# Backward products on the off-diagonal quarters, first output tile by single merged tiles, second down unit split early

## The reference

```python
def step(s0, inp):                       # one token of one direction; the scan runs forward and reversed
    r_t, w_t, k_t, v_t, kk_t, a_t = inp
    sa = einsum("bhvk,bhk->bhv", s, -kk_t)
    s = s * w_t[:, :, None, :] + sa[..., None] * (kk_t * a_t)[:, :, None, :] + v_t[..., None] * k_t[:, :, None, :]
    return s, einsum("bhvk,bhk->bhv", s, r_t)

merged = sigmoid(ga) * (attn_o @ w_attn_br) + sigmoid(gr) * (rwkv_o @ w_rwkv_br)
x = x + gate1 * (merged @ w_out)
h2 = modulate(rmsnorm(x, norm2_g), shift2, scale2)
up_u, up_g = split(dwconv3(h2 @ ffn_up, ffn_conv), 2)
x = x + gate2 * ((silu(up_g) * up_u) @ ffn_down)
```

## Time and profile before

| | |
|---|---|
| median of 3 runs | 1376.88 us (1375.66 to 1378.38) |
| profiled execution | 1380.84 us, its span 1379.1 us |
| mean granted clock of TensorE | 0.977 |
| PE busy | 1294.0 us, 13903 records |
| DVE / ACT / POOL busy | 689.9 / 550.1 / 42.1 us |
| first pass of the recurrence | from 320.3 us |
| second pass of the recurrence | from 589.2 us |
| output projection | from 782.5 us |
| down units | from 1192.4 us |

### The profile page before, as it was taken

One profiled execution on the slowest core, in us unless ns is written; L12 is line 12 of the kernel. 1 busy time (PEld: TensorE's weight loads), 2 busy tenths in 40 slices (PEclk: granted clock), 3 DMA queues, 4 the chain that ended last, 5 costly groups with the idle time before them and its releaser, 6 DMA issues.

```text
span 1379.1 us, 31730 instructions
## 1 busy us (share of the span) xinstructions
PE 1294.0 (94%) x13903; PEld 1196.7 (87%) x13903; DVE 689.9 (50%) x1036; ACT 550.1 (40%) x864; POOL 42.1 (3%) x103
## 2 busy tenths in 40 slices
PE   4899999998999769899999899899999999899996
PEld 1899999997999545499989788799999999899995
DVE  3437642642544676565556412654545545434544
ACT  4645534422233477533342121733334333233433
POOL 0100011000010000010000000000000000000000
PEclk9999999999999998999999999999999999999998
DMA  9322365315000200011017574021221211022222
GB/s 389 143 71 102 110 271 180 105 45 209 8 5 4 92 1 1 0 53 34 8 41 259 225 294 177 31 88 65 64 88 61 91 61 46 23 66 71 69 76 92
DMA packets 24027, 131.70 MB, mean 96 GB/s; under 512 B 2896, under 2 KB 3664, under 8 KB 15344
## 3 DMA queue, kind: packets, MB, share of 16 engines
q1 hardware_dynamic: 19104, 103.98, 21.5%
q0 software_dynamic: 4816, 26.11, 5.0%
HBM read 111.74 MB, written 18.34 MB: 94 GB/s over the span
## 4 chain that ended last, share of the span: by engine, by line
PE 60%; DVE 3%; ACT 2%; issue 1%; DVEq 0%; ACTq 0%
PE ps L712 30%; PE ps L1206 11%; PE ps L882 2%; PE ps L870 2%; PE ps L1093 1%; PE ps L850 1%; PE ps L737 1%; PE ps L756 1%; PE ps L1069 1%; PE ps L999 1%; PE ps L747 1%; DVE nmax L1972 1%; PE ps L1070 1%; PE ps L862 1%; PE ps L1040 1%
## 5 line engine op out<-in xcount | busy, mean ns | idle before, releaser
L712 PE MATMUL ps<-h2lo,whi 128*128 128x322 f32 x672 | 154.5, 311 | 0.7 <-ACT facc L1308 0.7
L712 PE MATMUL ps<-h2hi,wlo 128*128 128x322 f32 x672 | 155.0, 312 | 0.0
L712 PE MATMUL ps<-h2hi,whi 128*128 128x322 f32 x672 | 154.0, 310 | 0.0
L1662 DVE TENSOR_TENSOR wlo<-raw,whi 128x2048 fp32r<-128x2048 f32 x47 | 107.5, 2288 | 70.4 <-ACT whi L1269 70.4
L712 PE MATMUL ps<-hlo,whi 128*128 128x322 f32 x544 | 127.9, 316 | 1.0 <-ACT qkv L1334 1.0
L712 PE MATMUL ps<-hhi,wlo 128*128 128x322 f32 x544 | 125.4, 312 | 0.0
L712 PE MATMUL ps<-hhi,whi 128*128 128x322 f32 x544 | 124.7, 310 | 0.0
L712 PEld LDWEIGHTS ps<-h2hi,whi 128*128 128x128 f32 x672 | 114.2, 190 | 0.0
L712 PEld LDWEIGHTS ps<-h2lo,whi 128*128 128x128 f32 x672 | 113.0, 189 | 0.9 <-DVE wlo L1662 0.9
L712 PEld LDWEIGHTS ps<-h2hi,wlo 128*128 128x128 f32 x672 | 113.6, 189 | 0.0
L1709 DVE SCALAR_TENSOR_TENSOR facc<-fraw,par,facc 128x642 f32<-128x642 f32 x44 | 39.0, 887 | 138.7 <-ACT facc L1308 138.7
(11 more groups left out here) (339 smaller groups left out, 2596.7 us busy)
## 6 DMA issues: line engine op xcount, KB each, us to landing
raw<-in_wblk SPq DMA_DIRECT2D x48, 1024.0 KB, 4.9
adl<-in_wada SPq DMA_DIRECT2D x8, 2048.0 KB, 7.9
raw<-in_wdn SPq DMA_DIRECT2D x44, 256.0 KB, 2.6
adaw<-in_wada SPq DMA_DIRECT2D x4, 2048.0 KB, 20.7
gate_scratch<-gout POOLq DMA_DIRECT2D x16, 322.0 KB, 2.5
gld<-gate_scratch POOLq DMA_DIRECT2D x8, 644.0 KB, 4.6
attention_inputs_used<-attention_scratch SPq DMA_DIRECT2D x1, 5056.0 KB, 15.5
u_scratch<-uout POOLq DMA_DIRECT2D x12, 320.0 KB, 2.4
```

What stands on the lines that cost most here:

```text
L712: mm = pe.matmul(o, w, v, start=first, stop=last and w is hi and x is xh[n])
L1662: TT(wlo[s][:, :], raw[s][:, :], whi[s][:, :].bitcast(F32), ALU.subtract).then_inc(lo_done, 1)
```

## The change

Three edits.

**The recurrence.** The backward direction's H, G1 to G4, P and U go to the two off-diagonal quarters. H of d = 1 is written to the other 64 partitions and to the pair's second bank, so its copy in `hm` lies swapped. G of d = 1 takes R from those partitions and writes back to its own; so does U with P. Since R must lie on the other partitions for that, `rm` gets a third slot, and ACT fills it with two copies of 64 partitions each (stages X0 to X4, after R0 and V1 to V4). G5 writes d = 1's result straight to the third slot, on the diagonal. The loops over q and d are turned, so that four matmuls in a row name four different quarters. H1 now waits for `AK` and not for `T0`, since H writes where KA stood, and G waits for ACT's X and not for DVE's V. P0 takes over the wait for the last Y1.

**The merge.** The first output tile is written out as `out_first`: each k-tile waits for its own `mlo`. It no longer waits for the last branch tile's reading before it starts; `ada_late(4)` moves ahead of the last k-tile. The other seven tiles are as before.

**The MLP.** The second down unit is split ahead of the last up block too, into spare halves of the buffers of s = 0 (`dhi_second`, `dlo_second`, columns 512 to 1023 of `whi[0]` and `wlo[0]`).

```diff
-        rm[s] += [sb(f"rm{s}_{g}", [P, 2, 2, CH]) for g in range(2)]
+        rm[s] += [sb(f"rm{s}_{g}", [P, 3, 2, CH]) for g in range(2)]
...
-    AC_ST = ["P0", "H1", "U0", "H2", "P1", "H3", "U1", "Y1", "H4", "TR", "H5"]
+    AC_ST = ["P0", "X0", "H1", "U0", "H2", "X1", "P1", "H3", "X2", "U1", "Y1", "H4", "X3", "TR", "H5", "X4"]
...
-                gp.tensor_copy(rm[s][g % 2][:, :, :, :].rearrange("p d q n -> p (d q) n"),
+                gp.tensor_copy(rm[s][g % 2][:, 0:2, :, :].rearrange("p d q n -> p (d q) n"),
...
             elif name[0] == "H":
                 l = int(name[1])
-                dv("T0" if l == 1 else f"C{l - 1}")
-                for d in range(2):
-                    for q in range(2):
-                        for r in half:
-                            mm = pe.matmul(bank(b1, CH, CH * (2 * d + q))[r], abm[s][g % 2][r, d, q, 0, :], tm[s][r, d, q, :],
-                                           start=True, stop=True)
+                dv("AK" if l == 1 else f"C{l - 1}")
+                for q in range(2):
+                    for d in range(2):
+                        for r, away in zip(half, half[::-1]):
+                            mm = pe.matmul(bank(b0 + d, CH, CH * q)[away if d else r], abm[s][g % 2][r, d, q, 0, :],
+                                           tm[s][r, d, q, :], start=True, stop=True)
             elif name[0] == "G":
                 l = int(name[1])
                 ac(f"H{l}")
-                dv("AK" if l == 1 else f"V{l - 1}")
-                for d in range(2):
-                    for q in range(2):
-                        for r in half:
-                            left, right = rm[s][g % 2][r, d, q, :], hm[s][r, d, q, :]
+                ac(f"X{l - 1}")
+                for q in range(2):
+                    for d in range(2):
+                        for r, away in zip(half, half[::-1]):
+                            at = away if d else r
+                            turned, right = rm[s][g % 2][at, 2 * d, q, :], hm[s][at, d, q, :]
                             if l == 5:
-                                left, right = right, left
-                            mm = pe.matmul(bank(b0, CH, CH * (2 * d + q))[r], left, right, start=True, stop=True)
+                                mm = pe.matmul(bank(b0, CH, 4 * CH + CH * (2 * d + q))[at], right, turned, start=True, stop=True)
+                            else:
+                                mm = pe.matmul(bank(b0 + d, CH, 2 * CH + CH * q)[r], turned, right, start=True, stop=True)
             elif name[0] == "P":
                 if q == 0:
                     ac("TR")
+                    if g > 0:
+                        if g - 1 in ADDED:
+                            dv("Y1", g - 1)
+                        else:
+                            ac("Y1", g - 1)
                     if g == 1:
                         pe.wait_ge(sl_done, it + 1)
                     elif g > 1:
                         dv("S1", g - 1)
                 else:
                     dv("S0")
-                for d in range(2):
-                    for r in half:
-                        mm = pe.matmul(bank(b2, CH, CH * d)[r], akm[s][g % 2][r, d, q, 0, :], vt64[s][r, chunk_of(g, d, q), :],
-                                       start=True, stop=first)
-                    if not first:
-                        for r in half:
-                            mm = pe.matmul(bank(b2, CH, CH * d)[r], ar[s][r, d, chunk_of(g, d, q), 0, :], state(q)[r, d, :],
-                                           start=False, stop=True)
+                    if g == NG - 1:
+                        pe.wait_ge(pe_g[s], at_stage(PE_ST, it, g, "Y0"))
+                for n in range(1 if first else 2):
+                    for d in range(2):
+                        for r, away in zip(half, half[::-1]):
+                            left, right = (ar[s][r, d, chunk_of(g, d, q), 0, :], state(q)[r, d, :]) if n else \
+                                (akm[s][g % 2][r, d, q, 0, :], vt64[s][r, chunk_of(g, d, q), :])
+                            mm = pe.matmul(bank(b2 + d, CH, 6 * CH)[away if d else r], left, right, start=n == 0,
+                                           stop=first or n == 1)
             elif name[0] == "U":
                 ac(f"P{q}")
                 if q == 0:
                     dv("V5")
                 for d in range(2):
-                    for r in half:
-                        mm = pe.matmul(bank(b2, CH, P + CH * d)[r], rm[s][g % 2][r, d, q, :], pw[s][r, d, :], start=True, stop=True)
+                    for r, away in zip(half, half[::-1]):
+                        at = away if d else r
+                        mm = pe.matmul(bank(b2 + d, CH, 7 * CH)[r], rm[s][g % 2][at, 2 * d, q, :], pw[s][at, d, :], start=True,
+                                       stop=True)
...
-        pe.wait_ge(tile_evac, 2 * BLK_OUT + 2)
-        ada_late(4)
-        pe.wait_ge(m_lo, KD)
+        def out_first():
+
+            pe.wait_ge(lo_done, BLK_OUT + 1)
+            pe.wait_ge(hi_done, BLK_OUT + 1)
+            pe.wait_ge(tile_evac, 2 * BLK_OUT + 1)
+            for k in range(KD):
+                if k == KD - 1:
+                    pe.wait_ge(tile_evac, 2 * BLK_OUT + 2)
+                    ada_late(4)
+                pe.wait_ge(m_lo, k + 1)
+                hi, lo = (w[BLK_OUT % 2][:, k * 256:k * 256 + P] for w in (whi, wlo))
+                for q, (w, x) in enumerate(((hi, mlo[k]), (lo, mhi[k]), (hi, mhi[k]))):
+                    for o, v in zip(out_halves(0), halves(x)):
+                        mm = pe.matmul(o, w, v, start=k == 0 and q == 0, stop=k == KD - 1 and q == 2)
+            mm.then_inc(tile_done, 1)
...
+        out_first()
+        between_out(0)
+        pe.wait_ge(tile_evac, 2 * BLK_OUT + 2)
+        dense_tile(BLK_OUT % 2, 1, range(KD), mhi, mlo, out_halves(2), 256).then_inc(tile_done, 1)
+        between_out(1)
+        for b in range(BLK_OUT + 1, BLK_UP):
...
+            second = k == 1 and n == 1
             pe.wait_ge(d_hi, n + 1)
             pe.wait_ge(d_lo, n + 1)
+            xh, xl = (dhi_second, dlo_second) if second else (dhi[s], dlo[s])
             for f in (2, 3, 0, 1) if k == 0 and not again else range(4):
-                hi, lo = whi[s][:, f * P:f * P + P], wlo[s][:, f * P:f * P + P]
+                at = (4 + f if second else f) * P
+                hi, lo = (w[0 if second else s][:, at:at + P] for w in (whi, wlo))
                 outs = out_halves(2 * f, TP - 2)
                 if again:
                     pe.wait_ge(d_evac, f + 1)
                 if k == 0 and not again and f < 2:
                     pe.wait_ge(tile_evac, 2 * NBLK + 1 + f)
-                for q, (w, x) in enumerate(((hi, dlo[s]), (lo, dhi[s]), (hi, dhi[s]))):
+                for q, (w, x) in enumerate(((hi, xl), (lo, xh), (hi, xh))):
...
             for g, name, s in paired(AC_ST):
                 b0, b1, b2, b3 = range(4 * s, 4 * s + 4)
-                ac.wait_ge(pe_g[s], at_stage(PE_ST, it, g, name))
-                if name[0] == "H":
-                    ins = ac.activation(hm[s][:, :, :, :].rearrange("p d q n -> p (d q n)"), bank(b1, 4 * CH), ACT.Copy)
+                if name[0] == "X":
+                    ac.wait_ge(dv_g[s], at_stage(DV_ST, it, g, "R0" if name == "X0" else "V" + name[1]))
+                    for r, away in ((slice(0, 64), slice(64, 128)), (slice(64, 128), slice(0, 64))):
+                        ins = ac.activation(rm[s][g % 2][away, 2, :, :].rearrange("p q n -> p (q n)"),
+                                            rm[s][g % 2][r, 1, :, :].rearrange("p q n -> p (q n)"), ACT.Copy)
+                else:
+                    ac.wait_ge(pe_g[s], at_stage(PE_ST, it, g, name))
+                if name[0] == "X":
+                    pass
+                elif name[0] == "H":
+                    ins = ac.activation(hm[s][:, :, :, :].rearrange("p d q n -> p d (q n)"), ps[:, b0:b0 + 2, 0:2 * CH], ACT.Copy)
                 elif name[0] in "PU":
-                    dst, at = (pw[s], 0) if name[0] == "P" else (uw[s], P)
-                    ins = ac.activation(dst[:, :, :].rearrange("p d n -> p (d n)"), bank(b2, P, at), ACT.Copy)
+                    dst, at = (pw[s], 6 * CH) if name[0] == "P" else (uw[s], 7 * CH)
+                    ins = ac.activation(dst[:, :, :], ps[:, b2:b2 + 2, at:at + CH], ACT.Copy)
...
+            second = first and s == 1
+            ac.activation(whi[0][:, 512:1024] if second else whi[s][:, 0:512], raw[s][:, 0:512], ACT.Copy)
+            ac.activation((dhi_second if second else dhi[s])[:, :], af[:, k, :], ACT.Copy).then_inc(d_hi, 1)
 
         up_block(NBLK - 2, FF - 2, 0, False, False)
-        ac.wait_ge(act_done, 1)
+        ac.wait_ge(act_done, 2)
         ac.wait_ge(tile_done, 2 * NBLK - 2)
         down_hi(0, 0, 0, True)
+        down_hi(1, 1, 1, True)
         up_block(NBLK - 1, FF - 1, 1, False, False)
-
         ac.wait_ge(act_done, FF)
-        ac.wait_ge(tile_done, 2 * NBLK)
```

(16 more changed lines are left out.)

25 lines of the change are left out of this document (12 added, 13 removed).

## The result

The changed kernel takes 1420.24 us (median of 4, 1418.59 to 1421.63); beside it the kernel before took 1377.63. The ratio is 1.030, with a 95% interval from 1.028 to 1.0321: **43 us slower**, where 4 us faster was forecast. The time lies outside the predicted range.

A forecast was written before the change was run, and what follows sets the result against it. PE's queue was taken to bound the recurrence. Recurrence +6.2, merge -5.7, down unit -6.2 and clock +1.4 gave -4.3 us, so 1372.6 from the median 1376.88; range 1366 to 1382.

The forecast's parts named there:

- Four quarters at once: Chunk products on PE: four quarters run together at 0.0146 us a record, halving 11.2 us a group to 5.6.
- A: Recurrence on PE: off-diagonal quarters don't run beside the diagonal ones; net +28 us, 1405; chance 10%.
- B: Recurrence on PE: matmuls issue no faster than one per 0.025 us; net +15 us, 1392; chance 6%.
- The chunk stages through ACT: Recurrence: G waits for ACT's copies of R; +1.3 us a second-pass group, about nothing in the first, +6.2 in all.
- the walk: Step-by-step sum of waits and stage lengths through one second-pass group, from KB to KB; total +1.3 us.
- G2 to S1: Second-pass group, levels 2 and 3: this stretch goes from 4.30 us to 3.33.
- For PE falling to half clock: Recurrence: PE, now idling up to 2 us at a time, drops to half clock here and there; +1.4 us.
- rival C: Recurrence clock: a fall costs 1.7, perhaps 1.2 us; from five falls no gain, with seven groups +3, 1380; chance 14%.
- last sign of being wrong: Recurrence: the forecast is wrong if its clock row is under 0.95.
- The merge, -5.7: First output tile: starts right behind the branch tiles; 4.0 us from the gap and 1.7 from the clock.
- lands at 793, needed at 796.5: Merge: the ada load after ada 4, issued 5 us later, still arrives before PE needs it, so the gain stays.
- The second down unit, -6.2: MLP: the early split lets its 24 records fill PE's wait, so unit 2 starts 6.2 us earlier.

The follow-up runs named there:

- fill: The changed kernel plus identity products that nothing reads, issued where PE waits ahead of G and U1, first pair of heads only; 1411.0 us.
- Copies alone: The kernel before plus ACT's X copies with G waiting for them, all products still on the diagonal quarters, tails as before; 1446.6 us.
- half copies: The changed kernel with X1 to X4 copying only half of the columns, leaving part of R stale; 1409.2 us.
- copies early: The changed kernel with X1, X3 and X4 ahead of their level's H in ACT's order, X2 still behind H3, TR behind H5; 1373.1 us.
- last level: The changed kernel with off-diagonal quarters only for H5, G5, P and U, one X4 pair ahead of H5, H1 waiting for T0; 1362.5 us.

## Why the prediction was wrong

The forecast was +6.2 for the recurrence, +1.4 for the clock, -5.7 and -6.2 for the tails.

*Four quarters at once, 0.0146 us a record: right.* P's two rows of 8 records start 0.117 apart (705.47, 705.59 above), 0.0146 each. Rivals A and B are refuted. (Their prices would not have held by their own terms either: with six attention splits A's is some 4 us higher, and B's net comes to about +12, not +15.) B's rule in the Trainium skill (TensorE: Matmul & The Clock Gate, "Wait — 56ns, not 53.3ns?"), no start within some 25 ns of the last, does not hold for products on different quarters here.

*The chunk stages through ACT, +1.3 a group and +6.2 in all: this is the step that failed.* The path was right, G behind copies that stand behind both hm in ACT's queue; its length was not: a group of the second pass grew by 4.4 us at full clock (23.9 to 28.3) and not by 1.3. By the step's own terms, against the group shown above:

| step, us | before | forecast | measured |
|---|---|---|---|
| H2 to the first hm copy | 0.68 | 0.44 | 0.58 |
| both hm | 0.74 | 0.56 | 0.68 |
| attention split | 0.74 | 0.74 | 0.77 |
| X pair | | 0.46 | 0.65 |
| its end to G2 | 0.05 | 0.05 | 0.12 |
| H2 to G2 (level 2) | 1.11 | 2.25 | 2.80 |
| G2 to H3 | 1.92 | 1.1 | 1.37 |
| H3 to G3 (level 3) | 1.40 | 1.51 | 2.02 |

(Before, G2 waits for the hm copy of its own s alone, and neither for the split nor for an X pair.) The X pair is the largest single error: 0.46 came from copies that read PSUM, and even the upper bound, 0.60, was too low. The others are larger together: 0.14, 0.12, 0.03 and 0.07. Between the start of the second hm copy and the next instruction the walk had 0.28 us, as in the kernel before (639.39 to 639.67, where the next reads SBUF too); here it is 0.40 (702.62 to 703.02) and 0.41 (706.77 to 707.18), and no run tells why. Level 2 thus comes 0.55 late, level 3 0.51, level 4 likewise (711.58 to 714.39, 2.81 against 2.3), and G of s = 1 stands 0.66 behind the first, not 0.38. Level 5 makes 2.26 from H5 (718.46) to G5, for 1.80. These four levels are 2.0 us of the error, and some 0.2 to 0.3 comes behind each G of levels 2 to 4, whose second half is later. (Level 1 is apart: X0 stands ahead of H1, and H1 to G1 takes 1.49 for 1.40 before.) By subtraction the step was too small by 3.1 us a group: 28.3 with the fill at full clock, less 23.9 and 1.3. The first pass agrees: about nothing was forecast for a group without a split, and it takes 26.6 for 23.8 at full clock. Copies alone shows that both X pairs count and half copies fits it; copies early shows that their place matters and not their number. (The forecast's G2 to S1 adds up to 3.26 from its own terms, and not 3.33, which changes nothing.)

The forecast's own sentence "with X at 0.60 a pair the walk gives 6 more" shows how near the edge the walk was. PE's queue no longer covered the chain, so each 0.1 us in the four later levels was 4 us for the kernel. The range, which ended 9 us above the forecast, did not carry the hand-offs at all.

*For PE falling to half clock, 1.4: too small, and rival C's mechanism was real.* The rival needed five falls, and there are eight in the recurrence, 47.8 us at half clock against 6.8. It was priced at 1.7 us for a fall of 3.5 us; those here last 3.4 to 10.2. It adds 9 us or somewhat more (fill). With the rest of the forecast (-5.7) that alone would have made 3 us slower, not 43. The forecast's last sign of being wrong, a clock under 0.95 in the recurrence, did come: 0.94 and 0.90.

*The merge, -5.7.* The mechanism was right: from the branch tiles' end to the tile's end it takes about 9.5 us against 15.1, 5.5 less. The sentence "lands at 793, needed at 796.5" failed: the ada load comes 1.8 us after PE asks for it (845.86 above), where the kernel before has no such wait. Some 3 to 4 stay.

*The second down unit, -6.2.* Unit 0 to unit 2 takes 9.09 in place of 15.04: -5.95. The mechanism was right, and so was the size in the trace; the medians of the edit alone gave 3.3.

Both tails: -11.9 forecast, -9.4 in the trace, -9.5 and -7.7 by the medians.

## What to carry to other kernels

A copy that a product waits for has a price that depends on its place in its engine's queue: the same 200 copies cost 53 us over a kernel without them where they stood behind the operand that comes last, and 5 to 6 where most of them stood ahead of it. Before you take work from an engine that is 100% busy, measure how long the chain beside it is: here it was within two us a group of PE's queue, and the change added a wait (H1 for AK) to it, so 31 us taken from PE were worth under 2, while a part of them that puts nothing into the waits (the last level, P and U) was worth 7. And where the bound is a walk through hand-offs at 50 places, a forecast needs an error on each of them: 3 us a group was the larger part of this one's mistake, and the clock was most of the rest.

## What the runs showed of the hardware

- Four 64x64 quarters of the array take products at once: eight records of P start in 117 ns (705.47 to 705.59), where two diagonal quarters took four in that time.
- An ACT copy of 64x128 from SBUF to SBUF lasts 0.31 us and the next starts 0.32 after its start; of 64x64, 0.25 and 0.27. Copies of 128x128 that read PSUM start mostly 0.16 to 0.23 apart.
- Behind the second hm copy, an ACT instruction that reads SBUF starts 0.28 us after it in the kernel before (six of six), 0.40 to 0.42 in the changed kernel and in copies alone, and either of the two with the last level. No run tells what decides it.
- The granted clock went to half in the second pass of the changed kernel right behind three of six waits of 2.07 to 2.16 us, and in its first pass also in a row of waits of 1.25 (331 to 340 us); it stayed full in a group of the first pass with PE busy in 20 of 26.6 us:

```profile
372.10:398.70 26.60, 20.06 (x745) 18.82 (x742) 11.85 (x31) 12.77 (x42) 0.75 (x2) 1.00 0.02 4
```

- Open: the gaps of PE in which no engine is waited for. They are 15.4 us in the recurrence without copies, 5.8 with the last level alone, 7.0 before and 3.5 with the tails alone, whose recurrence is that of before. No run here tells what they are.
